# Turning the attention probabilities of the last two layers by VectorE and an exchange through memory

## The chip, the cores and the metric

One Trainium2 chip, one of its cores. The metric is the device time of one execution in microseconds (us). TensorE multiplies, VectorE, ScalarE and GpSimd work on tensors in the on-chip memory, and SyncE issues transfers. TensorE writes only to eight banks of 128 partitions x 512 fp32 numbers.

## The reference, cut to what matters

A first block (two mixers and two mixtures of experts) is followed by a second block of two layers. The change lies in the attention in the middle of each of these two layers: 8 neighbourhood heads and 8 sliding-window heads of width 64, over 256 tokens. Everything is fp32.

```
for l in range(DEPTH):
    x = x + 0.5 * swiglu(rms_norm_2(x, ffn1_norm[l]), ...)
    h = rms_norm_2(x, mix_norm[l])
    qa, ka, va, qs, ks_, vs, zg = split(h @ w_in[l])
    o_na = neighbourhood_attention(qa, ka, va, na_rpb[l])   # p = softmax(s + bias); o = p @ v
    o_sw = sliding_window_gqa(qs, ks_, vs, t5_bias, sw_sink[l])
    g = sigmoid(zg + b_gate[l])
    merged = g[:, :, 0] * (o_na @ w_branch_na[l]) + g[:, :, 1] * (o_sw @ w_branch_sw[l])
    x = x + merged @ w_out[l]
    x = x + 0.5 * swiglu(rms_norm_2(x, ffn2_norm[l]), ...)
```

The scores come out with queries on the partitions and keys along the row, since the softmax sums over keys in a row. The product with the values needs keys on the partitions, so each 256 x 256 matrix of probabilities must be transposed.

## The kernel before

**The stage.** In each layer `mixer_2` handles the 16 heads in eight rounds of two heads (`m` from 0 to 7, the first four neighbourhood heads). Round m also computes one eighth of the gate `zg` (`gates_first(m)` and `gates_rest(m)`, 28 products of 128 x 128 weights by 128 tokens, with the sums of weights of a seven-product (Strassen-like) scheme that GpSimd makes). A round of TensorE is, in order: `turned(m - 1)` (eight 128 x 128 transposes of the last round's probabilities through the identity), `scores(m)`, `values(m - 2)` (probabilities by values), `gates_first(m)`, `gates_rest(m)`. After the last round come `turned(7)`, `values(6)`, `branch(0, 0)`, `values(7)`, `branch(1, 0)` and the other branch products. `branch(p, n)` multiplies the attention's output by one part of `w_branch`.

**The other engines.** VectorE, in a round (`softmax(m)`, `gates(m)`): it adds the bias and takes the row's extreme (L3459), waits for ScalarE's exponentials, takes a reciprocal (L3468), scales the probabilities (L3471), then adds up the gate products from banks 4 and 5 (L3478 as soon as ScalarE has copied the first product, L3481 to L3485 after `gates_rest(m)`), and multiplies the gate by the inverse norm (L3488). ScalarE takes the exponentials (L2459), copies the transposed probabilities from the banks into `y.PT` (L2467), copies the values' products (L2471) and takes the gate's sigmoid (L2446). GpSimd only makes the sums of gate weights (L3572, four to a round, for round m + 1 as soon as round m - 1 has ended).

**What sets the order.** Every engine's order is written by hand, and an engine takes its instructions in that order. TensorE's `gates_first(m)` waits for `gate_sums` of m - 1 (L3485), because both use banks 4 and 5. SyncE has one queue for the stream of weights: each transfer of 1 MB (L844) waits until the chunk that had its place is used up (`to_be_free`), and during the rounds that is one transfer at the end of each round. The place is filled about ten chunks ahead of its use.

**A pattern used elsewhere.** The feed-forward stages turn their hidden values without TensorE: VectorE transposes blocks of 32 x 32 (L3277), ScalarE's queue writes them to memory (L2313), and reads them back in pieces of 128 bytes so that the blocks land in their transposed places (L2322).

## Time and profile before

| what | us |
|---|---|
| median of 3 runs | 2544.74 (2544.18 to 2547.61) |
| profiled execution, its own time | 2544.48 |
| its span, first to last instruction | 2543.2 |
| TensorE busy with matmuls | 2451.7 (96%) |
| rounds 1 to 7 of the first late layer | 65.0 |
| rounds 1 to 7 of the second late layer | the same rhythm of 9.4 a round |

A row of the timeline gives the start, the time until the end of the group, the engine and line, what is written and read, the count, and in brackets how long the engine had been idle and what released it. PEld rows are weight loads, which run just ahead of their matmuls and mark best where TensorE goes from one step to the next. A DMA row gives the time from issue to landing.

### The profile page before, as it was taken

How to read it: one execution, taken by the hardware profiler on the slowest of the kernel's cores; microseconds unless marked ns; L12 is line 12 of the kernel's file. 1: busy time of each engine (PE TensorE's matmuls, PEld its weight loads, DVE VectorE, ACT ScalarE, POOL GpSimd, SP SyncE). 2: the span in 40 equal slices, each digit the busy share in tenths (PEclk: the TensorE clock that was granted, in tenths of full speed). 3: DMA queues.
4: the chain of work that ended last, by engine and by line, in shares of the span. 5: the costliest groups of instructions: out<-in, count | busy, mean ns of one | idle time of the engine just before them, and what ended most of it. 6: DMA issues, size and time to landing. Idle time of an engine off the chain costs nothing.

```text
span 2543.2 us, 29763 instructions
## 1 busy us (share of the span) xinstructions
PE 2451.7 (96%) x12358; PEld 1567.5 (62%) x12358; DVE 1249.2 (49%) x2237; ACT 437.9 (17%) x1102; POOL 178.7 (7%) x126
## 2 busy tenths in 40 slices
PE   9999999888999999987889999999999999999999
PEld 5347443424578753332348866888866875888884
DVE  4994321212176621110117666545776775654774
ACT  2111110101123210000001002641101100470110
POOL 0011000000000000000000011430001003240000
PEclk9999999999999999999999999999999999999999
DMA  9854999999984499999999863415674974423671
GB/s 395 330 233 178 371 425 426 427 428 427 423 340 166 172 376 427 426 428 428 427 422 347 255 227 149 150 67 211 212 230 153 253 231 153 173 105 138 220 223 40
DMA packets 193618, 712.90 MB, mean 280 GB/s; under 512 B 117252, under 2 KB 121860, under 8 KB 128332
## 3 DMA queue, kind: packets, MB, share of 16 engines
q1 hardware_dynamic: 92304, 682.66, 67.6%
q10 hardware_dynamic: 101180, 28.35, 5.4%
q8 instruction: 98, 1.61, 0.3%
q14 instruction: 36, 0.29, 0.0%
HBM read 698.36 MB, written 12.60 MB: 280 GB/s over the span
## 4 chain that ended last, share of the span: by engine, by line
PE 79%; DMA 16%; DVE 4%; ACT 1%; issue 0%; POOL 0%; SPq 0%; another core or an unknown queue 0%; DVEq 0%; POOLq 0%
PE bank L867 77%; DMA ring<-in_stream 8%; DMA ring_high<-in_stream 4%; DMA ring_low<-in_stream 4%; PE bank L870 2%; DVE hidden L2892 1%; DVE ab_z L2717 1%; DMA hidden_turned<-normed 1%; DVE moe_results L2917 0%; POOL ab_ln_sum L3584 0%; DVE ring L3228 0%; DVE cd_y L2524 0%; DVE moe_turned L2913 0%; ACT normed L2243 0%; ACT hidden L2243 0%
## 5 line engine op out<-in xcount | busy, mean ns | idle before, releaser
L867 PE MATMUL bank<-ring,gates 128*128 128x256 f32 (+1 forms) x1760 | 433.6, 391 | 3.1 <-DVE ring L3228 2.1
L867 PE MATMUL bank<-ring,moe_chosen 128*64 128x512 f32 (+1 forms) x2352 | 400.3, 491 | 27.7 <-DMA ring<-in_stream 27.6
L867 PEld LDWEIGHTS bank<-ring,gates 128*128 128x128 f32 x1760 | 333.6, 190 | 70.7 <-issue 22.7
L867 PE MATMUL bank<-ring,normed 128*128 128x256 f32 x1448 | 339.6, 380 | 2.0 <-ACT normed L2328 1.3
L867 PEld LDWEIGHTS bank<-ring,moe_chosen 128*64 128x64 f32 x2352 | 150.6, 137 | 246.9 <-issue 200.4
L867 PEld LDWEIGHTS bank<-ring,normed 128*128 128x128 f32 x1448 | 273.1, 190 | 41.6 <-issue 3.9
L867 PE MATMUL bank<-normed,ring 128*128 128x256 f32 (+2 forms) x1152 | 289.8, 406 | 2.3 <-DVE normed L2698 1.5
L867 PEld LDWEIGHTS bank<-normed,ring 128*128 128x128 f32 x1152 | 189.4, 190 | 99.9 <-issue 85.4
L867 PE MATMUL bank<-ring,ffn_hidden 128*128 128x512 f32 (+1 forms) x416 | 179.3, 561 | 0.0
L2917 DVE COPY moe_results<-bank 32x512 f32<-32x512 f32 x36 | 24.8, 690 | 245.2 <-PE bank L867 244.8
L2908 DVE TENSOR_TENSOR moe_silu<-bank,moe_silu 128x512 f32<-128x512 f32 x32 | 22.1, 691 | 246.8 <-PE bank L867 246.8
L3228 DVE TENSOR_TENSOR ring<-ring,ring 128x1024 f32<-128x1024 f32 x117 | 142.1, 1215 | 1.6
L867 PE MATMUL bank<-ring,moe_turned 128*64 128x512 f32 x560 | 125.2, 595 | 17.4 <-DMA ring<-in_stream 14.3
L867 PEld LDWEIGHTS bank<-ring,ffn_hidden 128*128 128x128 f32 (+1 forms) x416 | 70.8, 182 | 86.3 <-issue 76.2
L2350 ACT ACTIVATE gates<-gates,small 128x256 f32<-128x256 f32 x88 | 44.4, 507 | 412.7 <-DVE gates L3241 226.2
L2164 ACT COPY moe_results<-bank 32x512 f32<-32x512 f32 x36 | 20.7, 575 | 467.1 <-PE bank L867 466.8
L867 PEld LDWEIGHTS bank<-ring,moe_turned 128*64 128x64 f32 x560 | 40.0, 137 | 98.6 <-issue 81.7
L2717 DVE SCALAR_TENSOR_TENSOR ab_z<-ab_pad_b,vectors,ab_z 128x512 f32<-128x512 f32 x120 | 90.2, 752 | 4.3
L3228 DVE TENSOR_TENSOR ring<-ring 128x1024 f32<-128x1024 f32 x71 | 85.8, 1208 | 0.0
L867 PE MATMUL bank<-ring,hidden 128*128 128x512 f32 x168 | 84.5, 592 | 0.0
L3308 DVE TENSOR_TENSOR ring<-ring 128x512 f32<-128x512 f32 x88 | 62.1, 705 | 38.2 <-PE bank L867 38.2
L3600 POOL TENSOR_TENSOR na_bias<-na_bias,na_mask 128x512 f32<-128x512 f32 x16 | 21.4, 1370 | 782.5 <-PE bank L867 782.5
(468 smaller groups left out, 2705.4 us busy)
## 6 DMA issues: line engine op xcount, KB each, us to landing
ring<-in_stream SPq DMA_DIRECT2D x318, 1024.0 KB, 7.3
ring<-in_stream SPq DMA_DIRECT2D x117, 2048.0 KB, 30.8
ring_low<-in_stream SPq DMA_DIRECT2D x7, 2048.0 KB, 43.8
ring_far<-in_stream SPq DMA_DIRECT2D x7, 2048.0 KB, 44.6
ring_high<-in_stream SPq DMA_DIRECT2D x6, 2048.0 KB, 44.8
hidden_turned<-normed ACTq DMA_DIRECT2D x44, 256.0 KB, 7.2
ffn_hidden<-hidden_turned ACTq DMA_DIRECT2D x44, 256.0 KB, 7.4
hidden<-in_stream SPq DMA_DIRECT2D x9, 1024.0 KB, 30.9
```

The lines of the kernel that those rows point to most:

```text
L867: return nc.tensor.matmul(o, lhsT, rhs, start=start, stop=stop, skip_group_check=True)
L870: return nc.tensor.transpose(o, x, ident[0:x.shape[0], 0:x.shape[0]])
L2164: ins = nc.scalar.copy(m.YG[CAP * e:CAP * e + CAP, i, 0:512], bank[4][CAP * i:CAP * i + CAP, :])
L2350: nc.scalar.activation(y.sg[:, t, :], (y.C2 if t else y.C1)[:, 0, :], ACT.Silu, scale=y.rinv_t[:, t:t + 1]).then_inc(*done.up((tag, l, "si ...
L2717: ins = v.scalar_tensor_tensor(out=z_j, in0=ab.PB[:, :, k:k + T], scalar=tap("conv_b", k, j), in1=z_j, op0=ALU.mult, op1=ALU.add)
L2892: v.scalar_tensor_tensor(out=H[:, s, n, :], in0=bank[5 + n % 3][:, T * i:T * i + T], scalar=M.MOD[:, l, 5, n, s:s + 1], in1=H[:, s, n, :], ...
L2908: v.tensor_tensor(m.SG, bank[1][:, :], m.SG, ALU.mult).then_inc(*done.up((tag, "hidden", g, e)))
L2917: ins = v.tensor_copy(m.YG[CAP * e:CAP * e + CAP, i, 512:1024], bank[4][64 + CAP * i:64 + CAP * i + CAP, :])
L3228: v.tensor_tensor(tw[:, i], a, b, ALU.subtract).then_inc(*done.up((tag, l, "t", c, i)))
L3308: v.tensor_tensor(to[:, i], a, b, ALU.subtract).then_inc(*done.up((tag, l, "dt", c, i)))
L3600: nc.gpsimd.tensor_tensor(part, part, mask, ALU.add).then_inc(*done.up(("na_bias", l, t) if h == NA_H - 2 else None))
```

## The change

**Transposes.** For rounds 0 to 6 TensorE no longer transposes. `y.SC`, the probabilities of both heads, is one buffer of 128 x 1024, laid out in pieces of 32 keys (`probs_of`). VectorE transposes it in 32 x 32 blocks into `y.turned` (`turned(m)`, one instruction, after it has scaled the probabilities). SyncE then writes `y.turned` to memory in four transfers of 32 partitions (pieces of 512 bytes, 512 KB in all), waits until they have landed, and reads it back in two transfers of 256 KB in pieces of 128 bytes into `y.PT` (`probs_exchanged`). The exchange of round m stands in SyncE's queue behind the weight transfer that waits for the end of round m. `turned(m)` of VectorE waits until the writes of m - 1 have landed, since `y.turned` is a single buffer. Round 7 keeps TensorE's transposes and ScalarE's copies.

**Order.** `values` runs three rounds behind instead of two (`LAG`), so `values(5)`, `values(6)` and `values(7)` come after the rounds, the last two one right after the other, behind `branch(0, 0)` and `branch(1, 0)`. The reversal of the queries moves from the copy of the probabilities to the copy of the output.

**Gates.** VectorE's sums of round m's gate (`gates_summed(m)`) move to the head of round m + 1. The product with the inverse norm moves to GpSimd (`gates_scaled`), behind the weight sums of two rounds later.

```diff
-    y.SC = [spare[:, 512 * n:512 * n + 512].rearrange("p (t k) -> p t k", t=TT) for n in range(2)]
-    y.PT = [[x[:, 512 * n:512 * n + 512].rearrange("p (k q) -> p k q", k=TT) for n in range(2)]
-            for x in (spare[:, 1024:2048], M.ring[WEIGHT_SUMS[0]][:, SLOT:SLOT + 1024])]
+    y.SC, y.turned = spare[:, 0:1024], spare[:, 1024:2048]
+    y.pairs = [M.ring[WEIGHT_SUMS[0]][:, SLOT + 1024 * n:SLOT + 1024 * n + 1024] for n in range(2)]
+    y.PT = [[x.rearrange("p (k i q) -> p i k q", k=TT, i=2)[:, i] for i in range(2)] for x in y.pairs]
...
+def probs_of(y, m, i, t):
+
+    order = "i t k f" if m == NA_H - 1 else "k i t f"
+    return y.SC.rearrange(f"p ({order}) -> p i t k f", i=2, t=TT, f=32)[:, i, t]
...
+    def probs_exchanged(l, m):
+
+        sp.wait_ge(*S.vector.at(("turned_2", l, m)))
+        if m >= 2:
+            sp.wait_ge(*S.probs_in.at((l, m - 2)))
+        for q in range(4):
+            rows = bass.AP(tensor=probs_blocks[m % 2].tensor, offset=q * 32 * 1024, ap=[[128, 32], [32 * 128, 8], [1, 128]])
+            nc.sync.dma_start(rows, M.late.turned[32 * q:32 * q + 32, :].rearrange("p (k n) -> p k n", k=8)).then_inc(
+                *S.probs_out.up((l, m) if q == 3 else None))
+        sp.wait_ge(*S.probs_out.at((l, m)))
+        if m >= 2:
+            sp.wait_ge(*S.tensor.at(("values_2", l, m - 2)))
+        for k in range(TT):
+            rows = probs_blocks[m % 2].rearrange("(q k p x f) -> k p x q f", q=4, k=TT, p=P, f=32)[k]
+            to = M.late.pairs[m % 2].rearrange("p (k x q f) -> p k x q f", k=TT, q=4, f=32)[:, k]
+            nc.sync.dma_start(to, rows).then_inc(*S.probs_in.up((l, m) if k == TT - 1 else None))
...
+    gate_chunks = {ring.index["in_2", l, 9 + m] + 1: (l, m) for l in range(LAYERS) for m in range(NA_H - 1)}
...
+        if ring.to_be_free(i, n) in gate_chunks:
+            probs_exchanged(*gate_chunks.pop(ring.to_be_free(i, n)))
...
+VALUES_AT = (6,) * (NA_H - 1) + (7,)
+LAG = 3
...
+            pe.wait_ge(*(A.at(("turned_2", l, m, 1)) if m == NA_H - 1 else S.probs_in.at((l, m))))
...
         pairs = NA_H
         for m in range(pairs):
-            if m:
-                turned(m - 1)
             scores(m)
-            if m >= 2:
-                values(m - 2)
+            if m >= LAG:
+                values(m - LAG)
             gates_first(m)
             gates_rest(m)
             if m == 1:
                 keys_turned()
         turned(pairs - 1)
+        values(pairs - 3)
+        branch(0, 0)
+        branch(1, 0)
         values(pairs - 2)
-        branch(0, 0)
         values(pairs - 1)
-        branch(1, 0)
         branch(0, 1)
         branch(1, 1)
         for p in range(2, KB // 2):
...
+            act.wait_ge(*S.pool.at(("gate", l, c)))
...
+        def turned(m):
+            dve.wait_ge(*done.at(("probs_2", l, m, 1)))
+            if m:
+                dve.wait_ge(*S.probs_out.at((l, m - 1)))
+            v.transpose(y.turned, y.SC).then_inc(*done.up(("turned_2", l, m)))
...
         for m in range(NA_H):
-            softmax(m)
+            if m:
+                gates_summed(m - 1)
+            biased(m)
+            probs(m)
+            if m < NA_H - 1:
+                turned(m)
+            gates_first(m)
             if m == 0:
                 keys_scaled()
             if m == 2:
                 keys_swapped()
-            gates(m)
+        gates_summed(NA_H - 1)
         dve.wait_ge(*A.at(("gate", l, KB - 1)))
         for p in range(KB // 2):
             for n in range(2):
...
+    def gates_scaled(l, c):
+        pool.wait_ge(*V.at(("gate_sums", l, c)))
+        by_block = y.gates_of[c].rearrange("p (n t) -> p n t", t=T)
+        nc.gpsimd.tensor_tensor(by_block, by_block, wide(y.rinv, 2), ALU.mult).then_inc(*done.up(("gate", l, c)))
...
+            if c >= 2:
+                gates_scaled(l, c - 2)
+        for c in (KB - 2, KB - 1):
+            gates_scaled(l, c)
...
```

VectorE's queue, second and third round of the first late layer (rounds 1 and 2). Before, from the end of round 1's probabilities to round 2's first bias (L3471 scales the probabilities, L3478 to L3485 are the gate's sums, L3488 its scaling, L3459 the bias):

```order
L3471 TENSOR_SCALAR hidden<-hidden,small 128x256
L3478 TENSOR_TENSOR ring_54<-bank,ring_54 128x2x128 [waits scalar_done]
L3481 TENSOR_TENSOR ring_54<-bank,ring_54 128x256 [waits vector_done,chunk_free]
L3483 TENSOR_TENSOR ring_54<-ring_54,bank 128x128 [waits vector_done]
L3485 TENSOR_TENSOR ring_54<-ring_54,bank 128x256 [waits vector_done]
L3488 TENSOR_TENSOR ring_54<-ring_54,late_rinv 128x512 [waits vector_done]
L3459 ISA hidden,small<-bank,na_bias 128x256 [waits tensor_done]
```

The same place of the changed kernel (L3508 scales, L3514 transposes, L3523 to L3533 are the sums, L3490 the bias; `out_probs` counts writes to memory that have landed):

```order
L3508 TENSOR_SCALAR hidden<-hidden,small 128x8x32
L3514 STREAM_TRANSPOSE hidden<-hidden 128x1024 [waits out_probs,vector_done]
L3523 TENSOR_TENSOR ring_54<-bank,ring_54 128x2x128 [waits scalar_done]
L3529 TENSOR_TENSOR ring_54<-bank,ring_54 128x256 [waits vector_done,chunk_free]
L3531 TENSOR_TENSOR ring_54<-ring_54,bank 128x128 [waits vector_done]
L3533 TENSOR_TENSOR ring_54<-ring_54,bank 128x256 [waits vector_done]
L3490 ISA hidden,small<-bank,na_bias 128x8x32 [waits tensor_done]
```

The transpose, with its wait for a transfer, stands ahead of the sums for which TensorE's `gates_first` waits, and the scaling is gone from this queue.

SyncE's queue in the changed kernel, from the weight transfer at the end of round 0 to the one at the end of round 2 (before, the weight transfers L876 stand alone, one behind the other):

```order
L876 DMA ring_50<-in_stream 128x2048 [waits chunk_free]
L846 DMA probs_turned<-hidden 32x8x128 [waits vector_done]
L846 DMA probs_turned<-hidden 32x8x128 x3
L854 DMA ring_53<-probs_turned 128x16x32 [waits out_probs]
L854 DMA ring_53<-probs_turned 128x16x32
L876 DMA ring_50<-in_stream 128x2048 [waits chunk_free]
L846 DMA probs_turned<-hidden 32x8x128 [waits vector_done]
L846 DMA probs_turned<-hidden 32x8x128 x3
L854 DMA ring_53<-probs_turned 128x16x32 [waits out_probs]
L854 DMA ring_53<-probs_turned 128x16x32
L876 DMA ring_51<-in_stream 128x2048 [waits chunk_free]
```

Four writes, a wait and two reads have come between each two transfers of weights.

TensorE's queue in the changed kernel, from behind the transposes of round 7 into the branch products (`ring_53,ffn_hidden` is `values`, `normed,ring_49` and `normed,ring_50` are the branch products with the two halves of the attention):

```order
L904 MATMUL bank<-ring_53,ffn_hidden 64x256 [waits in_probs,scalar_done]
L904 MATMUL bank<-ring_53,ffn_hidden 64x256 x3
L904 MATMUL bank<-normed,ring_49 128x256 [waits landed0]
L904 MATMUL bank<-normed,ring_49 128x256 x7
L904 MATMUL bank<-normed,ring_49 128x256 [waits scalar_done]
L904 MATMUL bank<-normed,ring_49 128x256 x7
L904 MATMUL bank<-ring_53,ffn_hidden 64x256 [waits in_probs]
L904 MATMUL bank<-ring_53,ffn_hidden 64x256 x3
L904 MATMUL bank<-ring_53,ffn_hidden 64x256 [waits scalar_done]
L904 MATMUL bank<-ring_53,ffn_hidden 64x256 x3
L904 MATMUL bank<-normed,ring_50 128x256 [waits scalar_done,landed2]
```

`values(6)` and `values(7)` stand one behind the other, and the branch product that follows waits for ScalarE's copy of the second.

## Rows read from the trace of the kernel before

**Rows 1.** The stage by windows: busy us and counts of each engine.

```profile
core 0: us, PE busy (x) PEld busy (x) DVE busy (x) ACT busy (x) POOL busy (x), PEclk, DMA share, GB/s
1619.60:1684.60 65.00, 65.00 (x557) 58.00 (x556) 40.38 (x144) 50.30 (x119) 32.10 (x24) 1.00 0.33 114
```

**Rows 2.** Timeline of one round, round 4: TensorE's weight loads.

```profile
1646.96 0.91 PEld L870 LDWEIGHTS bank<-kept,hidden 128*128 128x128 f32 x8
1648.03 0.73 PEld L867 LDWEIGHTS bank<-ffn_hidden 64*128 64x128 f32 x8 [0.17 <-issue]
1649.10 0.63 PEld L867 LDWEIGHTS bank<-hidden,ffn_hidden 128*64 128x64 f32 x8 [0.33 <-ACT ring L2467]
1650.11 1.86 PEld L867 LDWEIGHTS bank<-normed,ring 128*128 128x128 f32 x16 [0.39 <-issue]
...
1656.36 0.91 PEld L870 LDWEIGHTS bank<-kept,hidden 128*128 128x128 f32 x8
```

**Rows 3.** The same timeline, the sums of the gate on VectorE, and GpSimd.

```profile
1647.27 0.42 DVE L3481 TENSOR_TENSOR ring<-bank,ring 128x256 f32<-128x256 f32 x1 [1.49 <-PE bank L867]
1647.38 1.28 POOL L3572 TENSOR_TENSOR ring<-ring 128x512 f32<-128x512 f32 x1 [3.98 <-PE bank L867]
...
1648.05 0.42 DVE L3485 TENSOR_TENSOR ring<-ring,bank 128x256 f32<-128x256 f32 x1
```

**Rows 4.** Timeline around the end of round 0 and the start of round 1.

```profile
1617.60 0.61 DVE L3471 TENSOR_SCALAR hidden<-hidden,small 128x256 f32<-128x256 f32 x2
...
1619.38 0.41 DVE L3478 TENSOR_TENSOR ring<-bank,ring 128x256 f32<-128x256 f32 x1
1619.55 0.91 PEld L870 LDWEIGHTS bank<-kept,hidden 128*128 128x128 f32 x8
...
1621.69 1.86 PEld L867 LDWEIGHTS bank<-normed,ring 128*128 128x128 f32 x16 [0.33 <-issue]
```

**Rows 5.** Timeline after the last round: weight loads and ScalarE's copy.

```profile
1684.56 0.91 PEld L870 LDWEIGHTS bank<-kept,hidden 128*128 128x128 f32 x8
...
1685.63 0.63 PEld L867 LDWEIGHTS bank<-hidden,ffn_hidden 128*64 128x64 f32 x8 [0.17 <-issue]
...
1686.65 3.32 PEld L867 LDWEIGHTS bank<-normed,ring 128*128 128x128 f32 x16 [0.39 <-issue]
1686.76 0.37 ACT L2471 COPY normed<-bank 128x256 f32<-128x256 f32 x1 [0.39 <-PE bank L867]
...
1690.30 0.63 PEld L867 LDWEIGHTS bank<-ring,ffn_hidden 128*64 128x64 f32 x8 [0.33 <-issue]
```

**Rows 6.** Transfers, 1605 to 1700: issues with count, KB each, us to landing.

```profile
ring<-in_stream SPq DMA_DIRECT2D x11, 1024.0 KB, 4.8
```

**Rows 7.** One weight transfer alone, 1636 to 1644: busy tenths in slices of 0.2.

```profile
DMA  0000000000000090072889989989880300000000
```

**Rows 8.** One feed-forward exchange alone, 1443 to 1451, the same way.

```profile
DMA  0000000007999999000000000000199930096053
...
ffn_hidden<-hidden_turned ACTq DMA_DIRECT2D x1, 256.0 KB, 3.6
hidden_turned<-normed ACTq DMA_DIRECT2D x1, 256.0 KB, 2.0
```

**Rows 9.** The output's writes, 512-byte pieces, 2532 to 2540.

```profile
DMA  0000000000005999800000000000000299992699
...
out<-hidden SPq DMA_DIRECT2D x3, 256.0 KB, 2.3
```

**Rows 10.** Four reads of 64 partitions issued from 1384.4 to 1386.5: durations, landings.

```profile
L823 SPq DMA_DIRECT2D na_bias<-in_na_rpb x4: 601/643/791, 1384.4 to 1386.5; - x4
...
DMA to landing us min/median/max: 6.4/6.7/7.6
```

**Rows 11.** VectorE by line: the block transpose; the scaling beside GpSimd in round 1.

```profile
L3277 DVE STREAM_TRANSPOSE normed<-hidden x44: 711/711/712, 1366.2 to 2473.1; 128x512 f32<-128x512 f32 x44
L3471 DVE TENSOR_SCALAR hidden<-hidden,small x2: 388/872/1355, 1623.9 to 1624.3; 128x256 f32<-128x256 f32 x2
```

More of the change, by code:

```diff
@@ L1879, in values @@
                 pe.wait_ge(*V.at(("vs", l)))
-            for i in range(2):
-                pe.wait_ge(*A.at(("turned_2", l, m, i)))
+            pe.wait_ge(*(A.at(("turned_2", l, m, 1)) if m == NA_H - 1 else S.probs_in.at((l, m))))
             for k in range(TT):
@@ L1895, in branch @@
                 pe.wait_ge(*V.at(("gated", l, p - 2, n)))
+            elif p:
+                pe.wait_ge(*A.at(("turned_2", l, NA_H - 1, n)))
             for half in range(2):
@@ L2442, in gates @@
         def gates(c):
-            act.wait_ge(*V.at(("gate", l, c)))
+            act.wait_ge(*S.pool.at(("gate", l, c)))
             for half in range(2):
@@ L2483, in layer @@
                 keys_out()
+        values(NA_H - 3)
         turned(NA_H - 1)
+        gates(NA_H - 1)
         values(NA_H - 2)
-        gates(NA_H - 1)
         values(NA_H - 1)
@@ L3485, in gates @@
             v.tensor_tensor(to[:, 1:3, :], to[:, 1:3, :], d[:, 2:4, :], ALU.add).then_inc(*done.up(("gate_sums", l, c)))
-            dve.wait_ge(*done.now())
-            by_block = y.gates_of[c].rearrange("p (n t) -> p n t", t=T)
-            v.tensor_tensor(by_block, by_block, wide(y.rinv, 2), ALU.mult).then_inc(*done.up(("gate", l, c)))
         v.tensor_scalar(y.minus_sinks, M.sinks[:, l, :], -1.0, None, ALU.mult).then_inc(*done.up())
@@ L3613, in program @@
     pool_program(nc, a, M, S, ring)
-    every = [S.tensor, S.scalar, S.vector, S.pool, S.chunk, S.distance, S.spilled, S.hidden, S.sent, *S.landed, *S.into.values()]
+    every = [S.tensor, S.scalar, S.vector, S.pool, S.chunk, S.distance, S.spilled, S.hidden, S.probs_out, S.probs_in, S.sent, *S.landed, *S.into.values()]
     return {x.name: x.table for x in every}
```

52 lines of the change are left out of this document (30 added, 22 removed).

## Prediction, made before the changed kernel was run

> **What bounds the kernel now.** The windows view comes first: over rounds 1 to 7 of the first late layer TensorE is busy for all of the 65 us, VectorE for 40, ScalarE for 50, GpSimd for 32, and the transfers for a third of the time [rows 1]. So TensorE sets the pace, and what leaves its queue is worth its length until the next engine or queue is late. The timeline of one round then shows the steps by the starts of the weight loads [rows 2]: transposes 1646.96 to 1648.03 (1.07 us), scores to 1649.10 (1.07), values to 1650.11 (1.01), gate products to the next transposes at 1656.36 (6.25). A round is 9.40. Before the gate products may start, VectorE has to have finished the sums of the round before: it starts them 0.31 after the round's start (1647.27) and ends them at 1648.47, 1.51 after the start [rows 3]. TensorE comes to them at 3.15, so this wait is covered by 1.6 us. The other layer has the same rhythm, so I work out one layer and double it.
>
> **What the change takes away.** Seven of the eight transposes of a layer: 7 x 1.07 = 7.5 us on the path. If nothing else were late, the change would gain 15 us in two layers. The scaling of the gate leaves VectorE (0.7 us a round), which is not on the path. ScalarE loses seven pairs of copies, also off the path.
>
> **What it adds on TensorE and close to it.**
> (1) Round 1. VectorE ends round 0's probabilities at 1618.21, then does 1.2 us for the keys and starts the first gate sum at 1619.38 [rows 4]. Now a block transpose of 128 x 1024 comes first. The trace has 128 x 512 at 0.71 [rows 11]; twice that would be 1.42, and since part of it is fixed I take 1.25. So VectorE is done with transpose (1619.46), first sum (1619.85) and keys (1621.1) and ends the other sums at 1622.35. TensorE started those gate products at 1621.69 [rows 4]. Round 2 starts 0.65 later than before, where the absent transpose should have made it 1.07 earlier.
> (2) Round 2 loses its `values` as well (three rounds behind instead of two). Its gate products start at 1.55 after the round's start, held by the sums, not at 3.15. Of these 1.6 us 1.0 is only moved to the end. Rounds 3 to 7 have 0.5 us of cover left (2.08 against 1.51) and take 8.33 each if nothing else is late.
> (3) The end. Before, a branch product of 3.65 us stood between the steps: 1684.56, 1685.63, 1686.65, 1690.30 [rows 5]. Now `values(5)` is added here (1.0), `values(7)` follows `values(6)` at once and waits for ScalarE's copy of it, and the branch product after it waits for the next copy. Such a copy starts 0.11 after the next step's first load and takes 0.37 [rows 5], and with the release I count 0.55 for each wait. The end costs 2.1 more.
> With (1) to (3) alone round 2 starts at 1628.8, round 3 at 1636.6, and the transposes of round 7 at 1636.6 + 5 x 8.33 = 1678.25, against 1684.56: 6.3 less, with the end 4.2 less a layer, 8.4 us in all.
>
> **What it adds beside them: the exchange.** VectorE's transpose of round m waits until the writes of round m - 1 have landed. Behind this transpose stand the first gate sum (0.4) and the other three (1.2), and TensorE's gate products of round m + 1 wait for the last. So, with X(m) the time at which the writes of round m have landed, those gate products start no earlier than X(m - 1) + 1.25 + 0.4 + 1.2 = X(m - 1) + 2.9, and round m + 2 starts 6.25 after them. If the exchanges follow each other at a distance E that is longer than a round of TensorE, E becomes the round.
> All of it is in SyncE's one queue and goes through the same engines: weights (1 MB), writes (512 KB), a wait, reads (512 KB), the next weights. E from one landing of the writes to the next is a sum of data times and of one start and landing:
> - reads: a feed-forward read of 256 KB in the same pieces of 128 bytes landed after 3.6, with the transfer engines busy in 8 slices of 0.2, the first partly [rows 8]: 1.5 data, 2.1 start and landing. Two: 3.0.
> - weights: 1 MB landed after 4.8 [rows 6], busy for some 13 slices of 0.2 [rows 7]: 2.7. They can follow the reads at once.
> - writes: 256 KB in pieces of 512 bytes landed after 2.3, busy for five slices [rows 9]: 0.95. Twice: 1.9. But these writes come from 32 partitions each, and no row has that. The nearest other row, reads of 128 KB into 64 partitions in short pieces, landed from 1390.8 to 1394.1 for four, 1.1 each [rows 10], which gives 4.4 for four. I take 2.1, near the low end, because the piece and the direction are those of the output's writes.
> - start, landing and SyncE's waking: 2.1 + 0.1; by the writes' own row (2.3 less 0.95) it would be 1.4.
> E = 3.0 + 2.7 + 2.1 + 2.2 = 10.0; the low ends give 3.0 + 2.6 + 1.9 + 1.4 = 8.9, the high end of the writes 12.3.
> First landing: round 1 starts at 1619.55, SyncE issues the weights 0.3 later, they land after 4.8, and the writes end 2.0 behind them: X(0) = 1626.65. Then X(5) = 1626.65 + 5 x 10.0 = 1676.65, the gate products of round 7 start at 1679.55 and its transposes at 1685.8, 1.2 later than before. With the end (2.1) the layer is 3.3 us longer, and both 6.7. In general the layer changes by 5E - 46.8, which is zero at E = 9.35.
> The reads are not what is late: those of round 6 land some 5 us after X(6) = 1686.65, at 1691.8, and TensorE asks for them after transposes, `values(5)` and two branch products, at 1685.8 + 9.4 = 1695.2. That is a cover of 3.4. Later weight transfers slip by a few us, hidden by a ring filled ten chunks ahead.
> The moved product on GpSimd adds about 1.3 to its 5.1 a round (four sums of the size of one that took 1.28 [rows 3]), 6.4 of some 9. ScalarE's sigmoid waits for it and has room.
> Base: the profiled execution, 2544.5 (its median is 2544.7). 2544.5 + 6.7 = **2551**.
>
> The pieces of 128 bytes are the dear part: 1 MB moves in 2.7, and 512 KB of such pieces in 3.0 [rows 7, 8]. The Trainium skill (DMA: Bandwidth & Descriptors, Specifications) says that a transfer needs pieces of at least 512 B for line rate. At the weights' rate the two reads would be 1.35, and E 8.35, so TensorE would keep its pace and the result would be that of the first rival. The row, not the rate of large pieces, is taken.
>
> **The rivals.**
> *A. The exchange sets the round* (forecast, 67%). For it: the queue holds 7.8 us of data in a round of 8.3 and adds an idle time for the wait in the middle. With E from 9.1 to 11 it gives 2542 to 2561. Within it I give 5 to faster, 28 to no change, 34 to slower.
> *B. The exchange keeps up* (17%, faster). If reads and weights overlap more than the solo rows show, E is under 9.1, and the sum of (1) to (3) holds nearly or wholly: 2536. For it: a quick landing of small writes (2.0 [rows 8]). Against it: every piece of E was read from transfers that had the engines to themselves.
> *C. The scaling waits for GpSimd* (5%, no change). In round 1 one scaling of 128 x 256 took 1.36 beside another's 0.39, while GpSimd was at work [rows 11]. GpSimd's work now lasts until about 6.8 after the round's start, and the four scalings come while it runs. If each pays 1.0, a round of TensorE is held to about 9.4 by VectorE even if the exchange is quick: both layers keep the old rounds and pay the end, 2549. The Trainium skill (SBUF - State Buffer, Who interferes with whom) says that the two engines take a shared pair of ports for a whole instruction. By that rule the row is what should be seen, and in A the wait falls into the time in which VectorE waits for the writes anyway.
> *D. Writes from 32 partitions are as slow as the 64-partition reads* (6%, slower). E = 12.3: 14.7 a layer, 2574. It decides from E = 9.9 on, where the loss passes the 0.2% mark.
> *E. The last reads or the copies at the end are later than counted* (5%, slower). If the reads of round 6 land 5 us behind TensorE's question, 3 to 5 a layer: 2558.
>
> **How the numbers follow.** About 0.2% (5 us) is what a measurement of this kernel can tell from no change. Faster by more: 17 + 5 = 22%. Within: 28 + 5 = 33%. Slower by more: 34 + 6 + 5 = 45%. The range of the forecast's own case is 2542 to 2561; to leave out no more than 2 in 10 it has to take in most of B, so 2537 to 2562.
>
> **What would show it.** In the changed profile: weight loads of `scores` 9.6 to 10.4 apart from round 3 on (8.3 if B is right, 9.4 if C is); VectorE's transpose with idle time before it that a transfer ends, 1 us or more in rounds 3 to 6; TensorE's idle time before the first gate product released by VectorE's last sum; writes landing 7 after the weights' issue and two reads 5 after theirs; two gaps of about 0.5 around `values(7)`. A block transpose far from 1.25, or transposes without an idle time before them, would make the prediction wrong. So would reads that hold SyncE so long that its weight transfers come late.

## The result and the profile after

| what | before | changed |
|---|---|---|
| median | 2545.1 (2544.18 to 2547.61, 5 runs) | 2573.43 (2569.44 to 2578.15, 5 runs) |
| ratio to before, with its 95% interval | | 1.011 (1.0095 to 1.0125) |
| profiled execution: its own time, its span | 2544.48, 2543.2 | 2569.44, 2567.8 |
| first late layer: `scores(0)` to `turned(7)` | 72.3 | 81.5 |
| second late layer: the same | 72.3 | 84.3 |
| `turned(7)` to the start of `out_2` | 30.8 | 33.0 |

The change costs 28 us, 1.1%. The direction of the forecast was right and its mechanism was the one that acted, but the time lies far outside the range of 2537 to 2562.

SyncE's queue in the first layer (a row of the timeline: start, time for which the issues last, transfer, count). L854 are the two reads, and since SyncE waits for the writes' landing ahead of them, their starts are the X(m) of the prediction. L876 is the weights, L846 the four writes.

```profile
1619.04 0.33 SPq L876 DMA_DIRECT2D ring<-in_stream  x1
1619.41 2.58 SPq L846 DMA_DIRECT2D probs_turned<-hidden  x4
1626.36 1.98 SPq L854 DMA_DIRECT2D ring<-probs_turned  x2
...
1637.85 1.76 SPq L854 DMA_DIRECT2D ring<-probs_turned  x2
1639.65 1.70 SPq L876 DMA_DIRECT2D ring<-in_stream  x1
1641.47 2.30 SPq L846 DMA_DIRECT2D probs_turned<-hidden  x4
1648.55 2.04 SPq L854 DMA_DIRECT2D ring<-probs_turned  x2
...
1660.73 1.90 SPq L854 DMA_DIRECT2D ring<-probs_turned  x2
...
1673.30 1.92 SPq L854 DMA_DIRECT2D ring<-probs_turned  x2
...
1683.59 1.81 SPq L854 DMA_DIRECT2D ring<-probs_turned  x2
```

X(0) to X(5) is 57.23 us, so E was 11.45 and not 10.0. In the second layer X(0) is at 2232.70 and X(5) at 2291.41, which makes E 11.74. Over all six distances the means are 11.5 and 11.9, 11.7 for both layers; the experiments below are set beside that.

VectorE's block transposes and TensorE's wait, from the same timeline (in brackets how long the engine had been idle, and what released it). The gate products' first weight load is the row to set beside [rows 2].

```profile
1637.92 1.25 DVE L3514 STREAM_TRANSPOSE hidden<-hidden 128x1024 f32<-128x1024 f32 x1 [2.98 <-DMA probs_turned<-hidden]
...
1639.51 0.56 DVE L3479 COPY ffn_hidden<-ffn_hidden 64x256 f32<-64x256 f32 x1
...
1640.10 1.24 DVE L3480 COPY ffn_hidden<-ffn_hidden 64x256 f32<-64x256 f32 x1
...
1642.15 0.42 DVE L3533 TENSOR_TENSOR ring<-ring,bank 128x256 f32<-128x256 f32 x1
...
1642.68 3.49 PEld L904 LDWEIGHTS bank<-normed,ring 128*128 128x128 f32 x16 [5.13 <-issue]
1642.71 3.76 PE L904 MATMUL bank<-normed,ring 128*128 128x128 f32 x16 [4.70 <-DVE ring L3533]
```

The chain is the one forecast: X(1) at 1637.85, VectorE's transpose 0.07 later, its last sum ends at 1642.57, TensorE starts 0.1 later. From X(1) to the gate products it is 4.8 and not 2.9, because the two copies of keys (L3479, L3480), which come in this round only, stand in it; behind X(3), X(4) and X(5) it is 3.05. The transpose took the 1.25 us of the estimate. The idle times before the transposes of rounds 2 to 6 of the first layer are 2.98, 2.77, 1.18, 4.58 and 3.10 us, each ended by the writes.

How the transfer engines spend an exchange (busy tenths of all 16 engines). The first line is 1636 to 1648 in slices of 0.3 us, with X(1) at 1637.85 and X(2) at 1648.55; the second is 1660 to 1674 in slices of 0.35, with X(3) at 1660.73 and X(4) at 1673.30.

```profile
DMA  3111000000189999899999009999899689999842
```

```profile
DMA  1000006999799996047799996899962322100000
```

In the second, 1.4 us pass after the reads' issue, the reads fill ten slices (3.5), one is empty, weights and writes fill thirteen (4.55), then for five slices (1.75) only one to three tenths of the engines work, and 1.05 after that SyncE goes on. In the first, the reads fill twelve slices (3.6), weights and writes sixteen (4.8), and there is no such tail. Over the six exchanges of the first layer the engines are busy for 0.77 of the time.

The tail goes with the length of an exchange. With each of the twelve exchanges of both layers cut into forty slices, the three shortest (10.29, 10.70 and 10.77 us) end in 0.3 to 0.6 us of slices with only one to five tenths of the engines busy; the other nine, 11.4 to 12.9 long, in 0.8 to 3.2 us, and the longest exchange (12.91) has the longest tail.

### The profile page after: what moved, and what is told of

Its sections match the earlier page's. It is cut to its first block, busy times and chain, and to the rows that moved or that the text cites. A ratio compares the mean times of both kernels' runs of the same rounds, so it can differ in the third digit from the quotient of the medians.

```text
span 2567.8 us, 29623 instructions
## 1 busy us (share of the span) xinstructions
PE 2447.1 (95%) x12246; PEld 1563.6 (61%) x12246; DVE 1266.6 (49%) x2235; ACT 422.2 (16%) x1074; POOL 195.5 (8%) x142
## 4 chain that ended last, share of the span: by engine, by line
PE 73%; DMA 18%; DVE 6%; ACT 1%; SPq 1%; issue 0%; POOL 0%; another core or an unknown queue 0%; DVEq 0%; POOLq 0%
PE bank L904 72%; DMA ring<-in_stream 8%; DMA ring_high<-in_stream 4%; DMA ring_low<-in_stream 4%; DMA probs_turned<-hidden 2%; PE bank L907 2%; DVE hidden L2925 1%; DVE ab_z L2750 1%; SPq L846 1%; DMA hidden_turned<-normed 1%; DVE hidden L3514 1%; DVE hidden L3490 0%; DVE moe_results L2950 0%; ACT hidden L2494 0%; POOL ab_ln_sum L3644 0%
## 5 line engine op out<-in xcount | busy, mean ns | idle before, releaser
L904 PE MATMUL bank<-normed,ring 128*128 128x256 f32 (+2 forms) x1152 | 295.2, 413 | 30.8 <-DVE ring L3533 15.4
L904 PEld LDWEIGHTS bank<-normed,ring 128*128 128x128 f32 x1152 | 195.0, 197 | 128.9 <-issue 114.4
L904 PE MATMUL bank<-ring,ffn_hidden 128*128 128x512 f32 (+1 forms) x480 | 187.9, 539 | 0.9 <-ACT normed L2505 0.9
```

Source lines behind the costliest of these rows:

```text
L904: return nc.tensor.matmul(o, lhsT, rhs, start=start, stop=stop, skip_group_check=True)
```

## The experiments

All ratios are against runs of the kernel before on the same chip (median 2544.82 for `no_transfers`, `writes_first`, `two_buffers` and `scale_on_vector`, 2544.15 for `ends_covered` and `probs_on_scalar`, 2544.62 for the other four). Times are medians.

**Without the exchange.** What is the floor of terms (1) to (3)?

```diff
-            probs_exchanged(*gate_chunks.pop(ring.to_be_free(i, n)))
+            gate_chunks.pop(ring.to_be_free(i, n))
...
-            pe.wait_ge(*(A.at(("turned_2", l, m, 1)) if m == NA_H - 1 else S.probs_in.at((l, m))))
+            if m == NA_H - 1:
+                pe.wait_ge(*A.at(("turned_2", l, m, 1)))
...
-            if m:
-                dve.wait_ge(*S.probs_out.at((l, m - 1)))
```

> The six transfers of each exchange are left out and nothing waits for them; the values are multiplied by whatever lies in the buffer, so the output is not the reference's. VectorE's block transpose, the order, the lag of three and the scaling on GpSimd stay. Theory (the exchange's own cycle sets the rounds, and what was counted for TensorE's queue and its end was right): the floor of the prediction's first sum, about 2536 us (2533 to 2541), rounds 3 to 7 at 8.3 to 8.5 us, the end 2.1 us longer than before. Rival 1 (GpSimd's longer work holds VectorE's scalings, and so the rounds): rounds of 9.4 or more, 2549 or more. Rival 2 (the new order and lag cost more than counted): over 2545.

Measured: 2546.65 (2542.89 to 2553.14, 10 runs), ratio 1.0009 (1.0000 to 1.0018); profiled execution 2543.22. Without the exchange 27 of the 28 us of the loss are gone, and the interval of what is left begins at nothing; but the floor is the old time, not 2536. TensorE's weight loads in the first layer say where the expected gain went:

```profile
1636.20 0.73 PEld L904 LDWEIGHTS bank<-ffn_hidden 64*128 64x128 f32 x8
1637.27 0.63 PEld L904 LDWEIGHTS bank<-ring,ffn_hidden 128*64 128x64 f32 x8 [0.33 <-issue]
1640.53 1.86 PEld L904 LDWEIGHTS bank<-normed,ring 128*128 128x128 f32 x16 [2.63 <-issue]
...
1646.98 0.73 PEld L904 LDWEIGHTS bank<-ffn_hidden 64*128 64x128 f32 x8
```

Round 3 lasts 10.78, and the rounds 4 to 7 last 8.52, 8.59, 8.74 and 8.40, where 8.33 each was forecast: 3.4 us a layer. VectorE in the same kernel, from round 2 into round 3:

```profile
1631.81 1.96 DVE L3509 TENSOR_SCALAR hidden<-hidden,small 128x256 f32<-128x256 f32 x2
...
1633.88 1.43 DVE L3509 TENSOR_SCALAR hidden<-hidden,small 128x256 f32<-128x256 f32 x2
1635.35 1.25 DVE L3513 STREAM_TRANSPOSE hidden<-hidden 128x1024 f32<-128x1024 f32 x1
1636.52 0.38 DVE L3522 TENSOR_TENSOR ring<-bank,ring 128x256 f32<-128x256 f32 x1
1636.93 0.91 DVE L3480 COPY ffn_hidden<-ffn_hidden 64x256 f32<-64x256 f32 x1
1637.87 1.31 DVE L3481 COPY ffn_hidden<-ffn_hidden 64x256 f32<-64x256 f32 x1
1639.21 0.42 DVE L3528 TENSOR_TENSOR ring<-bank,ring 128x256 f32<-128x256 f32 x1
```

It is busy for 18.4 of the 20 us from 1617 to 1637 (14.4 in the kernel before), so VectorE is what is late here. Two things make it so. The two copies of keys stand ahead of the sums for which TensorE waits; the kernel before has them too, at 0.29 each, in a place where nothing waited. And whatever scales or copies while GpSimd works takes longer: a pair of scalings 1.96 instead of 0.61, the copies 0.91 and 1.31 instead of 0.29. That is the price of the rival C of the prediction, found on other work of GpSimd than the moved product.

**Writes ahead of the weights.** The same transfers, another order in SyncE's queue.

```diff
+    def probs_back(l, m):
+
         sp.wait_ge(*S.probs_out.at((l, m)))
...
+        exchange = gate_chunks.pop(ring.to_be_free(i, n), None) if ring.to_be_free(i, n) else None
+        if exchange:
+            probs_exchanged(*exchange)
...
-        if ring.to_be_free(i, n) in gate_chunks:
-            probs_exchanged(*gate_chunks.pop(ring.to_be_free(i, n)))
+        if exchange:
+            probs_back(*exchange)
```

`probs_exchanged` is now only the four writes; `probs_back` is the wait for them and the two reads. The weight transfer stands between the two.

> SyncE issues the four writes of round m ahead of the weight transfer that waits for the end of round m, and only the wait for their landing and the two reads behind it. Same transfers, same bytes. Theory (VectorE waits for writes that stand behind 1 MB of weights and in front of an idle start and landing): the writes land some 2.7 us earlier, and the weights fill the time that the wait leaves idle. A cycle of 3.3 (reads) + 2.7 (weights) + 2.7 (writes) + about 0.7 = 9.4 us in place of 11.5 to 11.9, so about 2545 us (2539 to 2553). Rival (what bounds the cycle is the bytes and pieces on the transfer engines, busy throughout): 2565 or more. Rival 1 (GpSimd): no change from 2573.

Measured: 2544.39 (2542.30 to 2546.05, 10 runs), ratio 0.9999 (0.9990 to 1.0008). It is as quick as no exchange at all: in the first layer TensorE's intervals equal those without transfers round for round within 0.02 us. The issues from 1605 to 1700 (count, KB, us to landing), first of the changed kernel, then of this one:

```profile
ring<-in_stream SPq DMA_DIRECT2D x9, 1024.0 KB, 7.1
probs_turned<-hidden SPq DMA_DIRECT2D x28, 128.0 KB, 5.4
ring<-probs_turned SPq DMA_DIRECT2D x14, 256.0 KB, 3.9
```

```profile
ring<-in_stream SPq DMA_DIRECT2D x11, 1024.0 KB, 5.3
probs_turned<-hidden SPq DMA_DIRECT2D x28, 128.0 KB, 2.3
ring<-probs_turned SPq DMA_DIRECT2D x14, 256.0 KB, 5.5
```

The writes land after 2.3 instead of 5.4 us, as the output's writes do in [rows 9], and the reads later, which nobody waits for. The engines are now busy for 0.94 of the time from 1629.8 to 1683.4. It is not that the engines have too much to do; it is that in the changed kernel the wait for the writes stands behind everything else, and the start and the landing are spent idle. With the writes first, 1 MB of weights runs while SyncE waits.

**A second buffer for the transposed blocks.** Is it VectorE's wait or SyncE's own loop?

```diff
-    y.SC, y.turned = spare[:, 0:1024], spare[:, 1024:2048]
+    y.SC, y.turned = spare[:, 0:1024], (spare[:, 1024:2048], gates[:, 3072:4096])
...
+            if c == 6:
+                act.wait_ge(*S.probs_out.at((l, 5)))
...
-            if m:
-                dve.wait_ge(*S.probs_out.at((l, m - 1)))
+            if m >= 2:
+                dve.wait_ge(*S.probs_out.at((l, m - 2)))
```

> VectorE's transpose writes to two buffers in turn, so that the transpose of round m waits for the writes of m - 2, not m - 1 (the second buffer lies where the gates of rounds 6 and 7 come later, so ScalarE's first gate copy of round 6 waits for the writes of round 5). Transfers and their order stay. Theory: VectorE's wait goes, but not the cycle of 11.5 us: rounds 1 to 5 run ahead until the lag of three rounds is used up, and then TensorE waits for the reads in values of rounds 4 to 6. About half of the loss comes back: 2559 us (2551 to 2567), with idle time of TensorE before the values, released by the transfers. If the cycle was long only because of the single buffer: 2545 or less.

Measured: 2569.59 (2563.98 to 2570.00, 4 runs), ratio 1.0099 (1.0082 to 1.0115): 10 us above what was expected, and above the range. VectorE no longer waits, yet the exchanges are 11.35 (from 1625.13 to 1693.25) and 11.1 apart in the two layers, 11.2 against 11.7, and `scores(0)` to `turned(7)` takes 80.5 against 81.5 in the first. The loop of SyncE keeps its length with nobody behind it. TensorE only waits in other places, now for the reads too:

```profile
1675.05 0.66 PEld L904 LDWEIGHTS bank<-ring,ffn_hidden 128*64 128x64 f32 x8 [2.52 <-issue]
1682.84 3.49 PEld L904 LDWEIGHTS bank<-normed,ring 128*128 128x128 f32 x16 [7.13 <-issue]
```

The 7.13 are partly of my own making: the second buffer lies in a part of the gates that ScalarE may fill only when the writes of round 5 have landed, and ScalarE waited 12.2 us for that. So this run shows that the loop is SyncE's; it doesn't give the price of a second buffer in a free place.

**The gate's scaling back on VectorE.**

```diff
-            act.wait_ge(*S.pool.at(("gate", l, c)))
+            act.wait_ge(*V.at(("gate", l, c)))
...
+            v.tensor_tensor(by_block, by_block, wide(y.rinv, 2), ALU.mult).then_inc(*done.up(("gate", l, c)))
```

> The scaling of the gate sums goes back to VectorE, behind the sums, as before the change; all else of the change stays. Theory (exchange): VectorE has idle time before its transpose, but the scaling stands between the gate sums and the bias at the head of the round, off that path: 2570 to 2576, as the change. Rival 1 (GpSimd's longer work holds VectorE): 2560 or less.

Measured: 2571.94 (2567.89 to 2573.52, 4 runs), ratio 1.0105 (1.0090 to 1.0120). The interval overlaps that of the changed kernel: no part of the move to GpSimd in the loss can be seen.

**The same at the floor**, where VectorE is late and it could matter: no exchange, and the scaling on VectorE.

> As the kernel without the exchange (no writes, no reads, no waits for them, so the value products use what is in the buffer), and in addition the gate sums are scaled by VectorE as before the change, so GpSimd is done 1.3 us earlier in a round. The kernel without the exchange measured 2546.65, no gain over the kernel before, though its rounds need only 8.33 us of TensorE. Theory: VectorE became what is late in rounds 1 to 3. It is busy without a gap there: the scaling of the probabilities takes 2.26, 1.96 and 1.43 us for a pair instead of 0.61 while GpSimd works at the differences for the gate, a work that both kernels have, and the two copies of keys take 2.2 instead of 0.6; moving the gate's scaling back frees at most one such wait in rounds 2 and 3 (0.8 us) and costs VectorE 0.69 a round. So 2544 to 2549, no difference. Rival: the product moved to GpSimd is what costs the gain; then 2538 to 2542, with TensorE's idle time of 2.63 us ahead of round 3's gate products down to under 1.

Measured: 2544.05 (2543.24 to 2549.94, 10 runs), ratio 1.0003 (0.9994 to 1.0012), and TensorE's wait ahead of round 3's gate products is 2.62 against 2.63. The pairs of scalings in rounds 1 and 2 got shorter (0.73 for 2.26, 1.75 for 1.96) and VectorE's own product ate what that gave.

**One read instead of two.**

```diff
-        for k in range(TT):
+        for k in range(1):
...
-            nc.sync.dma_start(to, rows).then_inc(*S.probs_in.up((l, m) if k == TT - 1 else None))
+            nc.sync.dma_start(to, rows).then_inc(*S.probs_in.up((l, m)))
```

> Only the first of the two reads of each exchange is made, so half of the transposed probabilities that the value products use are old ones; everything else is as in the changed kernel. Theory: the round is the length of SyncE's loop, in which the data of reads, weights and writes stand one behind the other and the wait for the writes' landing stands behind them all. SyncE does not wait for the reads, but their data delay the weights and the writes that are queued behind them. Two reads kept the transfer engines for about 3.3 us, so one less takes 1.65 off every round: reads issued about 9.8 us apart instead of 11.5, 5 x 1.65 x 2 = 16.5 us less than the changed kernel's 2573, that is 2556 (2550 to 2561). Rival: only the issue of the writes and their landing count, since SyncE passes the reads without waiting for them; then the distance stays above 11 and the time at 2568 to 2574. With the reads' landing on the path instead of their data, the same would be seen as in the rival, since one read lands as late as two.

Measured: 2555.08 (2552.61 to 2556.77, 4 runs), ratio 1.0040 (1.0025 to 1.0055), against 2556 expected. The exchanges are (1688.43 - 1624.59) / 6 = 10.6 and (2284.31 - 2225.85) / 6 = 9.7 us apart, 10.2 in the mean, 1.5 less than 11.7. In the first layer one of them took 13.5: there TensorE's slow gate products after its idle time freed the place of the weights only at about 1649.4, 4.8 after the reads. The reads do stand in the round although SyncE doesn't wait for them.

**Reads in pieces of 512 bytes.**

```diff
-            rows = probs_blocks[m % 2].rearrange("(q k p x f) -> k p x q f", q=4, k=TT, p=P, f=32)[k]
+            rows = probs_blocks[m % 2].rearrange("(q k p f) -> k p q f", q=4, k=TT, p=P, f=128)[k]
-            to = M.late.pairs[m % 2].rearrange("p (k x q f) -> p k x q f", k=TT, q=4, f=32)[:, k]
+            to = M.late.pairs[m % 2].rearrange("p (k q f) -> p k q f", k=TT, q=4, f=128)[:, k]
```

> The two reads of each exchange move the same 512 KB in pieces of 512 bytes instead of 128, so the probabilities lie in another order in the buffer and the value products are other ones; the number of bytes and of transfers is as in the changed kernel. Theory: the reads' data time is set by their number of pieces; at the rate of the weights (1 MB in 2.7 us) the two would take 1.35 instead of 3.3 us, the round 9.5 instead of 11.45, and the time 2573 - 10 x 1.95 = 2553 (2548 to 2559); the transfer engines are then busy for about 1.4 us behind the issue of the reads, not 3.3. Rival: the size of the piece does not matter here, the reads' time is that of the scattered access to memory; then 2568 to 2574.

Measured: 2566.61 (2565.07 to 2568.62, 4 runs), ratio 1.0087 (1.0072 to 1.0102). The median is 7 us less than the changed kernel's, not 20, and the two intervals touch (this one ends at 1.0102, that one begins at 1.0095); the rival's 2568 is nearer than the theory's 2553, though the time lies in neither range. The engines' time did go down: busy for 0.64 instead of 0.77 of the same stretch, which is about 1.5 us an exchange. But the exchanges are still (1695.25 - 1626.12) / 6 = 11.5 and (2299.70 - 2232.68) / 6 = 11.2 us apart, 11.35 in the mean, only 0.35 less than 11.7. One exchange, 1637 to 1649, in slices of 0.3; the reads were issued at 1638.14:

```profile
DMA  0000000268999950599997595699998444444320
...
ring<-in_stream SPq DMA_DIRECT2D x1, 1024.0 KB, 8.7
...
probs_turned<-hidden SPq DMA_DIRECT2D x4, 128.0 KB, 6.9
```

The reads are done in eight slices (2.4), and at the end of the writes there is a tail of eight slices (2.4) in which two to four tenths of the engines work. In this exchange what the shorter reads gave, the tail took. The Trainium skill (DMA: Bandwidth & Descriptors, Specifications) asks for 512 bytes for line rate, and for the reads' own engine time this run agrees (3.6 and 3.5 us in pieces of 128 bytes, 2.4 here). My expectation carried that over to the time of the kernel, with exchanges 9.5 apart, and the run shows 11.35. Why the tail is served by few engines is open.

**One write from 128 partitions instead of four from 32.**

```diff
-        for q in range(4):
-            rows = bass.AP(tensor=probs_blocks[m % 2].tensor, offset=q * 32 * 1024, ap=[[128, 32], [32 * 128, 8], [1, 128]])
-            nc.sync.dma_start(rows, M.late.turned[32 * q:32 * q + 32, :].rearrange("p (k n) -> p k n", k=8)).then_inc(
-                *S.probs_out.up((l, m) if q == 3 else None))
+        rows = bass.AP(tensor=probs_blocks[m % 2].tensor, offset=0, ap=[[128, P], [P * 128, 8], [1, 128]])
+        nc.sync.dma_start(rows, M.late.turned.rearrange("p (k n) -> p k n", k=8)).then_inc(*S.probs_out.up((l, m)))
```

> The four writes of 128 KB from 32 partitions each are one write of 512 KB from all 128 partitions, in the same pieces of 512 bytes but to other addresses, so the probabilities come back in another order; the rest is as in the changed kernel. Theory: a write's data time is that of its bytes and pieces; the engines were busy for 5.4 us with weights and writes together, 2.7 of them for the weights, so 2.7 for the writes, whatever their partitions. The distance stays within 0.6 us of 11.45, less only by the issues (four take 2.5 us now while the engines still work at the weights), and the time is 2567 to 2575. Rival: writes from 32 partitions are slow, as the fourth rival of the prediction had it; then one write takes 1.9 to 2.0, with 0.7 or more saved in a round, and the time is 2560 to 2566, or less.

Measured: 2577.66 (2571.18 to 2582.88, 4 runs), ratio 1.0131 (1.0107 to 1.0155), not quicker than the changed kernel, 2.7 above the expected range. The one write lands 8.0 us after its issue (6.9 to 9.2), and the exchanges are (1699.63 - 1628.57) / 6 = 11.8 and (2306.98 - 2237.63) / 6 = 11.6 apart, 11.7 in the mean as before. The tail is there too: in the exchange from 1640.44 to 1652.87 the last seven slices of 0.31 before the landing move only 31 to 18 GB/s. Writes from 32 partitions are not what is slow: the rival D is out, although its number, 2574, is nearly the measured time. Why the median is 4 us above the changed kernel's isn't settled; the two intervals overlap.

**A version that uses this.** Writes first, the copies of keys behind the biased scores of round 3, and an end in which a branch product covers each copy.

```diff
-            pe.wait_ge(*A.at(("out_2", l, m - 1) if m else ("va", l)))
+            pe.wait_ge(*A.at(("out_2", l, m - 1 if m < NA_H - 1 else m - 2) if m else ("va", l)))
...
-        branch(1, 0)
         values(pairs - 2)
         values(pairs - 1)
+        branch(1, 0)
...
+            if m == 3:
+                keys_swapped()
...
-            if m == 2:
-                keys_swapped()
```

> The changed kernel with the writes ahead of the weights in SyncE's queue, and in addition: VectorE's two copies of the keys stand behind the biased scores of round 3, not between round 2's first gate sum and its other sums; and at the end the order is values(5), a branch product, values(6), values(7), a branch product, where values(7) has a bank of its own and does not wait for ScalarE's copy of values(6). Theory: with the writes first the exchange is off the path, and what holds the kernel at the old time (2544.4) is VectorE in rounds 1 to 3 and the end. TensorE waits 2.64 us before round 3's gate products; without the copies (0.9 + 1.3 us beside GpSimd) ahead of the sums the wait is 0.5, and the copies fall into a stretch where VectorE waits for ScalarE, so 2.0 is gained. At the end the two waits of 0.93 and 0.99 become the usual 0.33 each, 1.2 less. 3.2 a layer, 6.4 in all: 2538 (2536 to 2541), a ratio to the kernel before of 0.9975. Rival: the VectorE work is only moved, the copies delay the scaling of round 3's probabilities, and round 4's gate products wait for it instead: then only the end is gained, 2542, and the wait of 2 us stands before the gate products of round 4.

Measured: 2537.33 (2535.09 to 2546.51, 12 runs), ratio 0.9972 (0.9963 to 0.9981). Both waits are gone, round 3's and those of the end:

```profile
1639.92 1.86 PEld L910 LDWEIGHTS bank<-normed,ring 128*128 128x128 f32 x16 [0.41 <-issue]
...
1686.55 1.49 PEld L910 LDWEIGHTS bank<-ring,ffn_hidden 128*64 128x64 f32 x16 [0.33 <-issue]
1688.43 24.04 PEld L910 LDWEIGHTS bank<-normed,ring 128*128 128x128 f32 x112 [0.39 <-issue]
```

**ScalarE divides the probabilities.** In addition to the last version, the four products of a round leave VectorE, and in round 0 VectorE scales the keys ahead of its transpose instead of behind it.

```diff
-                    v.tensor_scalar(part, part, total[:, t:t + 1], None, ALU.mult).then_inc(*done.up(("probs_2", l, m, i) if t else None))
...
+                    nc.scalar.activation(part, part, ACT.Identity,
+                                         scale=st[:, 4 + 2 * i + t:5 + 2 * i + t]).then_inc(*done.up(("probs_2", l, m, i) if t else None))
```

> As the kernel with the writes first, the late copies of the keys and the covered end, and in addition ScalarE divides the probabilities by their sums (four products of 128 x 256 a round), not VectorE, and in round 0 VectorE scales the keys while it waits for them. Theory: VectorE is what is late in rounds 1 to 3, 1.2 us a round for the scaling and up to 2.6 us more where a scaling meets GpSimd's work (1.65, 1.35, 0.8 and 1.8 us in rounds 1, 2 and 4). ScalarE has lost seven pairs of copies by the change and has room for four products of about 0.4 us. VectorE's waits go: round 1's gate products start about 0.2 earlier, those of round 2 at once behind the sums, and rounds 4 to 7 are 8.35 to 8.4 long instead of 8.4 to 8.75: about 1.2 a layer, 2.4 in all, so 2536 (2533 to 2539). Rival: ScalarE's products stand in the same chain from scores to transposed block and are longer than VectorE's (0.4 against 0.3 us), and VectorE was not the bound beyond the key copies: then no gain, 2538 to 2541.

Measured: 2534.59 (2533.25 to 2536.32, 5 runs), ratio 0.9962 (0.9950 to 0.9973), the quickest of all. TensorE no longer waits for VectorE in rounds 3 to 7, which now last 8.53, 8.52, 8.53, 8.52 and 8.33, where I had expected 8.35 to 8.4. So 8.52 is TensorE's own length of a round that is followed by `scores`. Its interval and that of the version before overlap; the traces show what it removes, and the size of that last step (2.7 us between the medians) is less certain than that both beat the kernel before. The two edits of this step were not run apart.

## Why the prediction was wrong, and where it was right

**The step that failed is the size of E**, "E = 3.0 + 2.7 + 2.1 + 2.2 = 10.0". The form of the sum was right: in "5E - 46.8" everything else can be read off the trace. From X(5) to the transposes of round 7 I had 2.9 + 6.25 = 9.15; both layers show 9.30 (1683.59 to 1692.89, 2291.41 to 2300.71). The end costs 2.16, I had 2.1. The excess over my 3.3 a layer is then

- first layer: 5 x (11.45 - 10.0) = 7.25, and X(0) 0.5 later after `scores(0)` than forecast (14.94 against 14.41), and 0.2 for the rest: 8.0, measured 9.15 + 2.16 - 3.3 = 8.0;
- second layer: 5 x (11.74 - 10.0) = 8.7, X(0) 1.9 later (16.29), and 0.2: 10.8, measured 11.98 + 2.16 - 3.3 = 10.8.

Both together, 18.8 us, are the miss of the profiled execution (2569.44 against 2551) within 0.4. The median of the changed kernel is 4 us above this execution.

**Which terms of E.** The two exchanges whose slices are shown above, term by term:

| term | forecast | X(1) to X(2) | X(3) to X(4) |
|---|---|---|---|
| reads | 3.0 | 3.6 | 3.5 |
| weights and writes, most engines busy | 4.8 | 4.8 | 4.55 |
| tail of the writes, few engines busy | none | none | 1.75 |
| start, gap, landing and waking | 2.2 | 2.3 | 2.8 |
| sum | 10.0 | 10.7 | 12.6 |

The data of weights and writes were right. The reads are 0.5 to 0.6 longer (and [rows 8] shows seven busy slices where I read eight, so my own row gave 2.8, not 3.0). The tail is what I had no term for, and so is the wait of SyncE for the place of the weights: 1.4 us from X(2) to X(3), told in the last section. No row of before could show the tail, because there no writes follow another transfer in the same queue: the landing of 2.3 in [rows 9] holds for writes that come first, as the kernel with the writes first shows. I had named the risk ("every piece of E was read from transfers that had the engines to themselves"), but only as an argument against the rival B. It was an argument for a wider range upward; I had put the high end of the forecast's own case at 11. What makes the tail stays open: neither the reads in longer pieces nor one write in place of four took it away.

One of the signs did not come as named either. From round 3 on the `scores` of the first layer start 16.1, 8.5, 9.8 and 14.0 apart, and the transposes of round 7 another 8.7 on, instead of 9.6 to 10.4 each: TensorE stood idle ahead of the gate products of rounds 3 to 7 for 5.13, 0.39, 1.60, 4.43 and 0.73 us. The exchanges set the sum of the rounds, not each of them.

**The rivals.** A was what happened. B's mechanism, an exchange that keeps up, is what the other order of the queue gives; its price of 2536, which already lay outside the range of 2537 to 2562, was wrong, since without an exchange the kernel takes 2546.65. C is out for the changed kernel, since it costs nothing to move the product back. But its price is real: GpSimd's older work, the sums of gate weights, holds VectorE up by 1.3 us for a pair of scalings. D gave nearly the measured number from a cause that is not there. E did not occur: the end is 2.16 longer.

**Terms (1) to (3).** (1) was right: the gate products of round 1 start 10.03 after `scores(0)`, before 9.45, so 0.6 later where I had 0.65. (3) was right. (2), "Rounds 3 to 7 ... take 8.33 each if nothing else is late", was wrong by 3.4 a layer: a round followed by `scores` instead of transposes lasts 8.52 (0.8 for four of them), and 2.3 are the wait of round 3, which is gone when the copies of keys no longer stand between the transposed block and the sums (`ends_covered`, where round 3 lasts 8.55). I had counted the block transpose ahead of the sums and overlooked two small instructions that stand there in one round of eight, and that they meet GpSimd. The rest, 0.3, is gone when ScalarE makes the scalings.

## What to carry to other kernels

When one queue carries a bulk transfer and a short one whose landing something waits for, issue the short one first: the same bytes here cost 29 us less (2544.39 against 2573.43), because the wait is spent on the bulk. A duration read from a transfer that is alone was too short here for the same transfer behind others, so such a sum needs its range upward. And when a step leaves the engine that sets the pace, list everything that the next engine has to do in its busiest round, once-only instructions included, before the gain is booked.

## What the runs showed of the chip

- Writes of 128 KB from 32 partitions land after 2.3 us when they lead in the queue and after 5.4 behind 1 MB of weights, in nine of the twelve exchanges of the changed kernel with a tail of 0.8 to 3.2 us in which half of the transfer engines or fewer work.
- On VectorE the scaling of 128 x 256 and the copy of 64 x 256 get longer beside GpSimd (0.61 for two to 1.96 and 2.26, 0.29 to 1.31), and so does a sum of two tiny operands (128 x 2): of eight in the changed kernel from 1619 to 1700 six took 0.15 or 0.16 us as before, the other two 0.64 and 1.21. The block transpose of 128 x 1024 took 1.25 every time, and the sums with one operand in a bank 0.42 every time, also beside GpSimd. The Trainium skill (SBUF - State Buffer, Who interferes with whom) names copies, scalings and sums of two operands in the on-chip memory as ones that can contend with GpSimd, and the traces agree; the transpose is not in its list.
- TensorE's clock. In the changed kernel TensorE stood idle for 5 us ahead of 1642.7, and in the stretch after it the granted clock was 0.63, with the first gate products at 3.49 for sixteen loads instead of 1.86:

```profile
1631.20:1637.50 6.30, 6.30 (x57) 5.66 (x57) 3.63 (x6) 4.74 (x10) 4.68 (x5) 1.00 0.71 242
1637.60:1642.60 5.00, 0.41 (x4) 0.00 (x0) 4.51 (x8) 0.00 (x0) 3.59 (x3) 0.92 0.90 131
1642.70:1650.80 8.10, 8.09 (x47) 8.10 (x48) 4.36 (x16) 3.73 (x11) 1.22 (x1) 0.63 0.67 198
1651.90:1661.00 9.10, 9.10 (x78) 8.00 (x78) 7.01 (x20) 7.02 (x17) 6.60 (x6) 1.00 0.75 197
```

(Columns as in [rows 1]; the clock is the third number from the right.) The value of 0.63 is a mean over the lower level (1.2 GHz), 0.50 from 1643 to 1648, and the upper (2.4 GHz), 1.00 from 1649 on. In the first layer this is not free. The slow products end at 1651.96, 3.4 us after X(2), where at the upper level (6.25 for a round's gate products) they would have ended at about 1648.9. SyncE has issued its reads by 1650.59 and then waits 1.4 us for TensorE to free the place of the weights:

```profile
1648.55 2.04 SPq L854 DMA_DIRECT2D ring<-probs_turned  x2
1652.06 0.36 SPq L876 DMA_DIRECT2D ring<-in_stream  x1
```

Between reads and weights the transfer engines then work at less than half for about 1 us, and this exchange took 12.18. How much of that is the clock's no run separates; it is at most these 1.4 us. In the second layer the slow products end at 2257.36, just before X(2) at 2257.61, and SyncE does not wait. The 9.30 from X(5) to the last transposes, at the upper level again, is the same in both layers.
